# A decoder layer in one program: the scheduler gets a table of hand-over latencies, the first weight tiles wait for input tiles, the late constants and two gate pieces change place

## The chip, the cores and the metric

The kernel runs on one Trainium2 chip, on all 8 cores. Every core computes the whole layer for one sequence of the batch, with no traffic between the cores. The time is the device time of the slowest core in microseconds. Of several executions the median is taken.

## What is computed

A hybrid decoder layer on x of 8 x 2048 x 1024 float32, cut to what matters here:

```python
x = x + 0.5 * swiglu(rmsnorm(x, ffn1_norm), w1, w3, w2)     # 1024 -> 2816 -> 1024
h = rmsnorm(x, mix_norm)
u = h @ w_in                                                 # q, k, v, ret gate, lru x, lru gate
ret = head_groupnorm(retention_chunkwise(rotary(q), rotary(k), v), ret_gn)
y_ret = (silu(g_ret) * ret) @ w_ret_o
hl = rg_lru(causal_depthwise_conv(x_lru, conv_w, conv_b), ...)
y_lru = (hl * gelu(g_lru)) @ w_lru_o
gates = sigmoid(h @ w_branch_gate + b_branch_gate)
x = x + (gates[..., :D] * y_ret + gates[..., D:] * y_lru) @ w_out
x = x + cross_attention(rmsnorm(x, xattn_norm), rmsnorm(mem, mem_norm))
x = x + 0.5 * swiglu(rmsnorm(x, ffn2_norm), ...)
out = rmsnorm(x, final_norm)
```

## The kernel before

Each core holds its sequence as 16 tiles of 128 tokens, in four blocks (tb) of 512. The program is recorded first as a list of operations with the memory that each reads and writes (`Prog.add`), and then put in an order for each engine by a list scheduler.

**The scheduler.** `Prog.schedule` plays the program through with a cost for each operation. Of the operations whose inputs are there it takes the one that can start first on its engine, and among equals the one with the longest path behind it. It also gives out the 8 PSUM banks. What an operation of another engine waits for is taken to be ready `SEM_NS` = 70 ns after its end, whatever the two engines are. A DMA costs its bytes by `DMA_NS_PER_B` plus `DMA_LAT`. Three passes more use the due times of the pass before (`latest`) as keys of the DMAs. The pass with the shortest modelled span gives the order, and that order is fixed in the program: each engine works strictly through its list, POOL (GpSimd) and SP (SyncE) with the DMAs that they issue in it too.

**FFN, up stage** (`FFN.up`, `unit`). The product with W1 and W3 is done for two blocks at a time by a scheme that needs 7 products where 8 are plain. A product is four matmuls of 128x512 (L751, `bank<-hTh,WS` or `bank<-SUM,WS`). A unit is one hidden chunk m of 22 for one pair p of blocks: 7 products, 28 matmuls, on three banks. Three of them go to one bank after another, with a copy of the bank by ACT (L767, `EV<-bank`) in between, so the next product of that bank waits for the copy; others wait for an addition on DVE (L1062). The weights of chunk m lie in one of five slots (`NSLOT`, tiles `WS`): two halves loaded by POOL's queue (L780, 512 KB in HBM each), and four subtractions (L1017, `WS<-WS`), on DVE for the first `TDVE` = 2 chunks and on POOL for the rest. `SUM` tiles are sums over halves of the normalised input (`sums`, L1033). Pair 0 runs `LEAD` = 3 units ahead of pair 1.

**Start.** SP loads the 16 tiles of x and the row of norm weights. ACT squares and sums (`n1JK`), POOL raises to the power -1/2 (`stat`, L949), DVE scales (`n1HB`, L957), PE transposes (L970). `load13` takes for the first three chunks a list of x tiles that must have landed before the halves are loaded; chunks 3 and 4 have no such list.

**Constants.** `consts_late` makes masks, decay tables and bias columns: some 90 small operations, most of them on DVE (L825 to L890), recorded behind the norm of the first FFN.

**FFN, down stage** (`FFN.down`): 704 matmuls `bank<-W,HID`, in pairs of banks for each token tile; at tiles 4 to 11 it carries one of eight side jobs (four `rope_piece`, four `centre_v`). The weights W of this stage and the first weights of the mixer (`LW`) are loaded by POOL's queue.

**Mixer.** 16 steps u of the recurrent branch (`stA`, `stB`, `stG`; `XL`, `XC`, `XCB`, `LW`) run interleaved with the retention steps (`qk`, `gate_`, `block`; weights `RW`), with 16 pieces of the branch gates (`gate_piece`, weights `GW`; `GSCHED` says how many after which step) and the products for the memory attention (`mem_jobs`, `XW`). A tile of the normalised input comes into `hT` by a DMA transpose on SP's queue for tiles below `TR1` = 16, so for all of them. Then come the output products (`tail`, weights `TW`), the cross-attention and the second FFN.

Of the kernel before, what the change touches and what calls it, by code (L numbers as in the profile page):

```python
# [20 lines left out]
SEM_NS = 70.0  # L21
DMA_NS_PER_B = 1.0 / 300.0
DMA_LAT = 2500.0
# [46 lines left out]
class Prog:  # L70
# [42 lines left out]
    def schedule(self, plan=None):  # L113
# [10 lines left out]
        for op in reversed(ops):  # L124
            m = 0.0
            for x in op.succ:
                if bl[x.id] > m:
                    m = bl[x.id]
            bl[op.id] = m + op.cost + (DMA_LAT if op.dma else 0.0)
            op.key = -bl[op.id]  # L130
        for op in ops:
            if op.tie is not None:
                op.key = min(op.key, op.tie.key)
        if plan is not None:
# [33 lines left out]
        def can_take(op):  # L168
# [12 lines left out]
            return b, freeat[b] + SEM_NS  # L181
# [8 lines left out]
        def dma_gate(op):  # L190
# [4 lines left out]
            for x in w:  # L195
# [3 lines left out]
                t = x.fin + SEM_NS  # L199
# [32 lines left out]
        while n:  # L232
# [83 lines left out]
    def latest(self, plan):  # L316
# [14 lines left out]
        for op in sorted(ops, key=lambda o: (-st[o.id][0], -o.id)):  # L331
            dur = op.cost + op.dma * DMA_NS_PER_B + (DMA_LAT if op.dma else 0.0)
            m = span - dur
            for x in op.succ:
                v = ls[x.id] - (0.0 if x.eng == "pe" and op.eng == "pe" else SEM_NS) - dur
                if v < m:
                    m = v
            for i in later[op.id]:
                v = ls[i] - SEM_NS - dur
# [230 lines left out]
TR1 = 16  # L570
# [6 lines left out]
GSCHED = [0, 1, 1, 1, 1, 2, 2, 1, 1, 1, 1, 1, 1, 1, 1, 0]  # L577
# [3 lines left out]
LEAD = 3  # L581
TDVE = 2
# [43 lines left out]
def record(stage, plan):  # L626
# [90 lines left out]
    IOI = A.buf("IOI", 136 * KB, I32, 256)  # L717
    IOF = A.buf("IOF", 137 * KB, F32, 3 * 256)
    WVS = A.buf("WVS", 8 * KB, F32, KC * 256)
    WVB = A.buf("WVB", 16 * KB, BF16, KC * 256)  # L720
    WVM = A.buf("WVM", 20 * KB, F32, KC)
# [33 lines left out]
    def act(out, in_, func, reads, writes, n, tab=None, bias=None, scale=None, accum=None):  # L755
# [8 lines left out]
        if accum is not None:  # L764
            kw["accum_out"] = accum
            nap += 1
# [44 lines left out]

    io_i = IOI.v()
# [15 lines left out]
    def consts_late(gate):  # L828
        dve(lambda e: e.memset(onesb.ap, 1.0), [], onesb.hs, 128)

# [167 lines left out]
    class FFN:  # L998
# [3 lines left out]
        def __init__(self, which):  # L1002
            self.which = which
            self.n13 = 0
            self.units = 0

        def load13(self, after=((), ())):
# [8 lines left out]
            for d, x, y in ((t3, b22, b12), (b12, b12, b11), (t2, b22, b12), (t4, b21, t2)):  # L1016
# [76 lines left out]

        def up(self, side=()):
            bk = Banks(P, 2)
            side = list(side)
            self.sums(0)
            done = [0, 0]

            def go(p):  # L1100
# [3 lines left out]
                self.unit(m, p, bk)  # L1104
# [5 lines left out]
            self.sums(1)  # L1110
            while done[1] < NM:
# [739 lines left out]
```

How the kernel before makes its waits and increments, by code:

```python
            def run(ename, eng):  # L441
                waited = {}
                for op in order[ename]:
                    ws = {}
                    for d in waits[op.id]:
                        if d.dma:
                            s, v = dsem[d.eng][d.idx % NDMASEM], 16 * (d.idx // NDMASEM + 1)
                        else:
                            s, v = esem[d.eng], d.semval
                        if waited.get(id(s), 0) >= v:
                            continue
                        waited[id(s)] = v
                        ws[id(s)] = (s, v)
                    for (s, v) in ws.values():
                        eng.wait_ge(s, v)
                    if op.fn is None:
                        continue
                    ins = op.fn(eng)
                    if op.dma:
                        ins.then_inc(dsem[ename][op.idx % NDMASEM], 16)
                    elif op.marked:
                        ins.then_inc(esem[ename], 1)
```

## Time and profile before

| | |
|---|---|
| median of 3 runs | 1794.6 us (1788.92, 1794.6, 1797.78) |
| the profiled execution | 1786.93 us, span of its slowest core (core 7) 1785.6 us |
| spans of the 8 cores | 1770.6 to 1785.6 us |
| PE busy | 1658.7 us, 93% of the span, 7928 matmuls |
| DVE, ACT, POOL busy | 51%, 44%, 40% of the span |
| chain that ended last | PE 80%, DMA 6%, issue 5%, DVE 4%, ACT 3%, POOL 2% |

An engine's busy time is the time in which it has an instruction in work. Matmuls overlap: one of 128x512 is shown as 379 ns long, while the next one may start much earlier, so short waits of PE are partly hidden in its busy time. The granted clock (PEclk) is 1.00 for 2.4 GHz and 0.50 for 1.2 GHz; in between it is a mean over a stretch.

### The profile page before, as it was taken

The numbers are of one execution on the slowest core, as the hardware profiler recorded it, in microseconds if no ns is written. First come the engines' busy times: TensorE is split into PE (matmuls) and PEld (weight loads), VectorE is DVE, ScalarE is ACT, GpSimd is POOL, SyncE is SP. The second block draws the span as 40 slices with busy tenths as digits, with TensorE's granted clock in tenths as the row PEclk, the third lists the DMA queues.
The fourth block names the chain that finished last, engine by engine and source line by source line (L and its number), as shares of the span: only waits on it lengthen the run. The fifth ranks groups of instructions, "written<-read, shape, count | busy, mean of one in ns | idle before, by whom it ended". The sixth has DMA issues, their size and how long they took to land.

```text
span 1785.6 us, 24375 instructions; the slowest of 8 cores (1770.6 to 1785.6 us)
## 1 busy us (share of the span) xinstructions
PE 1658.7 (93%) x7928; PEld 756.0 (42%) x7928; DVE 911.9 (51%) x1306; ACT 791.2 (44%) x1258; POOL 718.8 (40%) x715
## 2 busy tenths in 40 slices
PE   2899999999979998999997988999999999999998
PEld 1443344344434544444443433444444444444443
DVE  5845644358566544656656423366476444442322
ACT  4544444212146675485675623335444444442111
POOL 5566565401135433443534424323015666653000
PEclk9999999999999998999999999999999999999999
DMA  9232223878984555732101366164444323246332
GB/s 230 54 48 42 30 42 60 141 192 238 204 154 78 94 102 101 162 68 52 38 22 24 67 170 159 36 212 84 134 135 104 42 39 45 42 66 129 131 118 83
DMA packets 111756, 177.27 MB, mean 99 GB/s; under 512 B 49680, under 2 KB 61968, under 8 KB 109584
## 3 DMA queue, kind: packets, MB, share of 16 engines
q0 software_dynamic: 31680, 62.40, 24.1%
q1 hardware_dynamic: 79952, 113.31, 21.0%
q8 instruction: 66, 1.08, 0.2%
q14 instruction: 58, 0.48, 0.1%
HBM read 185.64 MB, written 41.94 MB: 127 GB/s over the span
## 4 chain that ended last, share of the span: by engine, by line
PE 80%; DMA 6%; issue 5%; DVE 4%; ACT 3%; POOL 2%; DVEq 0%; POOLq 0%; ACTq 0%; SPq 0%
PE bank L751 78%; DMA WS<-f_w 2%; DMA XW<-w_xqT 1%; DVE EV L1062 1%; POOL ATP L1530 1%; DMA CS<-rope 1%; DMA W<-f_w 1%; DVE XC L1317 0%; DMA LW<-w_lru_in 0%; ACT L767 0%; PE bank L970 0%; DMA RW<-w_g 0%; DMA XW<-w_xk 0%; DMA TW<-w_tail 0%; POOL QK L1398 0%
## 5 line engine op out<-in xcount | busy, mean ns | idle before, releaser
L751 PE MATMUL bank<-hTh,WS 128*128 128x512 f16 x1408 | 339.5, 382 | 8.6 <-DVE cst L889 2.6
L751 PE MATMUL bank<-W,HID 128*128 128x512 bf16 x1408 | 306.2, 380 | 3.4 <-DMA W<-f_w 3.4
L1062 DVE TENSOR_TENSOR EV<-bank,EV 128x512 f32<-128x512 f32 x264 | 181.8, 690 | 225.9 <-PE bank L751 138.7
L751 PE MATMUL bank<-SUM,WS 128*128 128x512 f16 x1056 | 264.0, 380 | 10.4 <-ACT EV L767 3.7
L751 PEld LDWEIGHTS bank<-hTh,WS 128*128 128x128 f16 x1408 | 136.5, 98 | 183.0 <-issue 27.4
L1017 POOL TENSOR_TENSOR WS<-WS 128x512 f16<-128x512 f16 x160 | 193.5, 1211 | 46.8 <-DMA WS<-f_w 31.6
L751 PEld LDWEIGHTS bank<-W,HID 128*128 128x128 bf16 x1408 | 138.0, 98 | 171.3 <-issue 6.7
L767 ACT ACTIVATE EV<-bank 128x512 f32<-128x512 f32 x264 | 155.5, 590 | 105.3 <-PE bank L751 100.1
L949 POOL TENSOR_TENSOR stat<-stat,cst 128x1 f32<-128x1 f32 x82 | 53.4, 653 | 358.8 <-DVE stat L948 358.6
L767 ACT ACTIVATE EV<-EV 128x512 f32<-128x512 f32 x176 | 110.5, 629 | 192.9 <-DVE EV L1062 188.2
L751 PEld LDWEIGHTS bank<-SUM,WS 128*128 128x128 f16 x1056 | 95.8, 97 | 157.0 <-issue 58.7
L1092 POOL TENSOR_TENSOR HID<-EV,EV 128x512 bf16<-128x512 f32 x88 | 112.2, 1276 | 104.4 <-ACT EV L767 103.1
L751 PE MATMUL bank<-hT,GW 128*128 128x512 bf16 x512 | 121.3, 386 | 7.2 <-DVE GU L1559 3.0
L751 PE MATMUL bank<-hT,RW 128*128 128x512 bf16 x512 | 117.0, 380 | 7.0 <-ACT RS L767 3.3
L751 PE MATMUL bank<-hT,LW 128*128 128x512 bf16 x512 | 116.9, 383 | 6.0 <-DVE T L1395 5.1
L1317 DVE SCALAR_TENSOR_TENSOR XC<-XL,pc,XC 128x1024 f32<-128x1024 f32 x48 | 66.8, 1391 | 68.9 <-ACT XL L767 67.1
L1141 DVE SCALAR_TENSOR_TENSOR XR<-bank,XR 128x512 f32<-128x512 f32 x64 | 43.0, 687 | 103.9 <-PE bank L751 97.9
L1085 DVE TENSOR_TENSOR HID<-bank,EV 128x512 bf16<-128x512 f32 x88 | 60.7, 690 | 54.9 <-PE bank L751 53.0
L1615 DVE SCALAR_TENSOR_TENSOR TT<-TT,bank 128x512 f32<-128x512 f32 x64 | 43.6, 687 | 79.3 <-PE bank L751 73.8
L751 PEld LDWEIGHTS bank<-hT,GW 128*128 128x128 bf16 x512 | 50.0, 99 | 67.4 <-issue 14.7
L751 PEld LDWEIGHTS bank<-hT,RW 128*128 128x128 bf16 x512 | 49.7, 98 | 66.6 <-issue 10.7
L751 PEld LDWEIGHTS bank<-hT,LW 128*128 128x128 bf16 x512 | 50.0, 98 | 65.5 <-issue 9.1
(192 smaller groups left out, 2263.0 us busy)
## 6 DMA issues: line engine op xcount, KB each, us to landing
WS<-f_w POOLq DMA_DIRECT2D x88, 256.0 KB, 4.4
W<-f_w POOLq DMA_DIRECT2D x44, 256.0 KB, 4.9
X<-x SPq DMA_DIRECT2D x16, 512.0 KB, 8.5
XR<-x SPq DMA_DIRECT2D x16, 512.0 KB, 4.8
park<-XR SPq DMA_DIRECT2D x16, 512.0 KB, 4.9
gate_scr<-GU SPq DMA_DIRECT2D x64, 128.0 KB, 2.1
GIN<-gate_scr SPq DMA_DIRECT2D x8, 1024.0 KB, 6.4
X<-park SPq DMA_DIRECT2D x16, 512.0 KB, 5.1
```

Source lines behind the costliest of these rows:

```text
L751: ins = e.matmul(out_ap, l, r, start=(start and i == 0), stop=(stop and i == n - 1), skip_group_check=skip)
L767: P.add("act", lambda e: e.activation(out, in_, func, **kw), reads=reads, writes=writes, cost=act_cost(n, nap), tab=tab)
L949: pool(lambda e: e.tensor_tensor(s[:, 2:3], s[:, 1:2], cc(2), ALU.pow), hs + cst.hs, hs, 550)
L1017: f = (lambda e, d=d, x=x, y=y: e.tensor_tensor(d.ap, x.ap, y.ap, ALU.subtract))
L1062: dve(lambda g: g.tensor_tensor(e.ap, banks[bank][:, :], e.ap, ALU.add), [hbk[bank]] + e.hs, e.hs, TB)
L1085: dve(lambda g: g.tensor_tensor(ha, bv, e1v, ALU.mult), [hbk[al]] + e1.hs, hha, TB)
L1092: pool(lambda g: g.tensor_tensor(hb_, e2v, e4v, ALU.mult), e2.hs + e4.hs, hhb, pool_cost(TB))
L1141: dve(lambda e, b=bs[half], xv=xv: e.scalar_tensor_tensor(xv.ap, banks[b][:, :], 0.5, xv.ap, ALU.mult, ALU.add), [hbk[bs[half]]] + xv.hs, ...
L1317: dve(lambda e, s=s: e.scalar_tensor_tensor(xc.ap, XL.v(s, 1024).ap, pcol("conv_w", s * 8 + c), xc.ap, ALU.mult, ALU.add), xl_all.hs + xc. ...
L1530: pool(lambda e, sa=sa, da=da, rb=rb: e.tensor_tensor(da, sa, rb, ALU.mult), src[0].hs + src[1].hs + rs.hs, dh_[0].hs + dh_[1].hs, pool_co ...
L1615: dve(lambda e, t=t, by=by: e.scalar_tensor_tensor(t.ap, t.ap, 1.0, banks[by][:, :], ALU.add, ALU.mult), t.hs + [hbk[by]], t.hs, TB)
```

## The change

Five edits. (1) The scheduler takes the hand-over time from a table by pair of engines, where it took 70 ns for all: 262 ns from PE to ACT, 272 ns from PE to DVE, 146 ns from any engine to PE, 60 ns within an engine, 100 ns behind a DMA. It takes DMAs as slower too. (2) All five first chunks of weights wait for x tiles (`G13`), and their 20 subtractions are on DVE (`TDVE` = 5, before 2, which made 8). (3) `consts_late` becomes the first side job of the down stage, and every other side job moves back by one token tile; the scratch tiles of the two move to free memory. (4) Pair 0 of the up stage leads by 4 units (`LEAD`). (5) Two gate pieces get their own space and are recorded ahead of step 0 (`EARLY`), and `GSCHED` takes them from steps 1 and 2. The last two tiles of `hT` are transposed by PE (`TR1` = 14). `plain`, `NPLAIN`, `SEED` and `JIT` are switched off.

```diff
-SEM_NS = 70.0
-DMA_NS_PER_B = 1.0 / 300.0
-DMA_LAT = 2500.0
+DMA_NS_PER_B = 1.0 / 240.0
+DMA_LAT = 3000.0
+LAT = {("pe", "act"): 262.0, ("pe", "dve"): 272.0, ("act", "dve"): 140.0, ("dve", "act"): 95.0, ("dve", "pool"): 145.0,
...
+def lat(op, eng):
+    if op.dma:
+        return 100.0
+    if op.eng == eng:
+        return 0.0 if eng == "pe" else 60.0
+    if eng == "pe":
+        return 146.0
+    return LAT.get((op.eng, eng), 280.0 if op.eng == "pe" else 150.0)
...
-                lat = 0.0 if (s.eng == "pe" and e == "pe") else SEM_NS
-                if end + lat > s.ready:
-                    s.ready = end + lat
+                w = end + lat(op, s.eng)
+                if w > s.ready:
+                    s.ready = w
...
-TR1 = 16
+TR1 = 14
...
+EARLY = 2
-GSCHED = [0, 1, 1, 1, 1, 2, 2, 1, 1, 1, 1, 1, 1, 1, 1, 0]
+GSCHED = [0, 0, 0, 1, 1, 2, 2, 1, 1, 1, 1, 1, 1, 1, 1, 0]
...
-LEAD = 3
-TDVE = 2
+LEAD = 4
+TDVE = 5
+G13 = [(1, 3), (5, 6), (7, 8), (9, 10), (12, 14)]
...
-    for i, o in enumerate((56, 16, 96)):
+    for i, o in enumerate((56, 16, 96, 24, 32)):
...
-    f1.load13((x0(1).hs, x0(3).hs))
-    f1.load13((x0(5).hs, x0(5).hs))
-    f1.load13((x0(7).hs, x0(7).hs))
-    gate = x0(15).hs
+    for i, j in G13:
+        f1.load13((x0(i).hs, x0(j).hs))
...
-    consts_late(gate)
...
-    side = []
+    side = [lambda: consts_late([])]
...
+    for i in range(EARLY):
+        gp(*pieces.pop(0), 3 + i)
```

What the change does to the order is seen at three places. The first is POOL's list at the start of the program (WS_51 to WS_55 are the five weight slots, chunk 0 in WS_51; f_w the weights in HBM; stat the powers of the norm). Before:

```order
L780 DMA WS_54<-f_w 128x1024 x2
L780 DMA WS_55<-f_w 128x1024
L818 IOTA IOI 128x128
L837 IOTA IOI 128x16
L857 IOTA IOI 128x1
L780 DMA WS_55<-f_w 128x1024
L1017 TENSOR_TENSOR WS_54<-WS_54 128x512
L949 TENSOR_TENSOR stat<-stat,cst 128x1 x2
L780 DMA WS_51<-f_w 128x1024
L1017 TENSOR_TENSOR WS_54<-WS_54 128x512 x2
L949 TENSOR_TENSOR stat<-stat,cst 128x1
L1017 TENSOR_TENSOR WS_55<-WS_55 128x512
```

And of the change:

```order
L843 IOTA IO_98 128x128
L975 TENSOR_TENSOR stat<-stat,cst 128x1
L804 DMA WS_51<-f_w 128x1024
L975 TENSOR_TENSOR stat<-stat,cst 128x1 x2
L804 DMA WS_51<-f_w 128x1024
L975 TENSOR_TENSOR stat<-stat,cst 128x1 x2
L804 DMA WS_52<-f_w 128x1024
L975 TENSOR_TENSOR stat<-stat,cst 128x1
L804 DMA WS_52<-f_w 128x1024
L975 TENSOR_TENSOR stat<-stat,cst 128x1
L804 DMA WS_53<-f_w 128x1024
```

Before, the halves of chunks 3 and 4 go first, ahead of those of chunk 0, and their subtractions stand among the powers. In the change the halves come in the order of the chunks, one by one between the powers, and no subtraction stands there.

The second place is PE's list in the steady part of the first up stage (bank numbers shown; SUM0 and SUM1 belong to pair 0 and pair 1, WS0 to WS4 are the slots). Before:

```order
L751 MATMUL bank1<-hTh_46,WS3_54 128x512 x4
L751 MATMUL bank5<-SUM1_58,WS0_51 128x512 x4
L751 MATMUL bank1<-SUM0_57,WS3_54 128x512 x4
L751 MATMUL bank7<-hTh_46,WS0_51 128x512 x4
L751 MATMUL bank1<-SUM0_57,WS3_54 128x512 x4
L751 MATMUL bank4<-hTh_46,WS3_54 128x512 x4
L751 MATMUL bank3<-hTh_46,WS3_54 128x512 x4
L751 MATMUL bank6<-hTh_46,WS1_52 128x512 x4
L751 MATMUL bank3<-hTh_46,WS3_54 128x512 x4
L751 MATMUL bank6<-SUM1_58,WS1_52 128x512 x4
```

And of the change:

```order
L775 MATMUL bank3<-SUM1_58,WS0_51 128x512 x4
L775 MATMUL bank2<-hTh_46,WS4_55 128x512 x4
L775 MATMUL bank1<-hTh_46,WS4_55 128x512 x4
L775 MATMUL bank6<-hTh_46,WS1_52 128x512 x4
L775 MATMUL bank3<-SUM1_58,WS0_51 128x512 x4
L775 MATMUL bank7<-SUM0_57,WS4_55 128x512 x4
L775 MATMUL bank6<-SUM1_58,WS1_52 128x512 x4
L775 MATMUL bank5<-hTh_46,WS1_52 128x512 x4
L775 MATMUL bank7<-SUM0_57,WS4_55 128x512 x4
L775 MATMUL bank6<-SUM1_58,WS1_52 128x512 x4
```

Before, one product stands between two on the same bank (bank 1, bank 3, bank 6). In the change there are at least two. Counted over a whole up stage, a product with only one other between it and the one whose bank had to be copied or added first comes 71 times in the first FFN and 76 times in the second before, and 2 times and never in the change. The price is that three units are open at a time, where two were.

The third place is PE's list where the mixer starts, behind the last product of the down stage. Before:

```order
L751 MATMUL bank<-hT,LW 128x512 x16
L751 MATMUL bank<-hT,RW_120 128x512 x32
L751 MATMUL bank<-XCB,LW 128x512 x4
L751 MATMUL bank<-hT,LW 128x512 x32
L751 MATMUL bank<-hT,RW_120 128x512 x32
L751 MATMUL bank<-RW_120,hT 128x512 x8
```

And of the change:

```order
L775 MATMUL bank<-hT,LW 128x512 x16
L775 MATMUL bank<-XCB,LW 128x512 x4
L775 MATMUL bank<-hT,LW 128x512 x16
L775 MATMUL bank<-hT,GW_147 128x512 x16
L775 MATMUL bank<-hT,LW 128x512 x8
L775 MATMUL bank<-hT,RW_121 128x512 x32
L775 MATMUL bank<-hT,GW_147 128x512 x8
```

The 32 matmuls of RW that stood between the first 16 of LW and the 4 on XCB have moved behind them, and the early gate pieces (GW_147, and GW_149 further on) stand among the rest.

In POOL's list for the down stage, four loads of LW stood among the loads of W before, three of them ahead of its last eight. In the change all of W is loaded first. In the output products, the last 48 matmuls of gate pieces in one row are now split in rows of 16 and 24, and between the last of them and the first use of the weights TW that are loaded behind them there are now 16 matmuls, where there were 8.

## Rows read from the trace of the kernel before

**Rows 1.** Stretches, core 7: length, busy (count) by engine, PEclk, DMA share, GB/s.
```profile
45.00:75.00 30.00, 25.89 (x150) 12.43 (x151) 28.64 (x37) 18.23 (x32) 14.55 (x14) 0.91 0.23 68
75.00:170.00 95.00, 93.10 (x417) 38.88 (x416) 43.00 (x66) 44.17 (x76) 59.10 (x58) 1.00 0.28 40
170.00:200.00 30.00, 24.42 (x102) 9.61 (x101) 25.96 (x77) 13.94 (x24) 18.16 (x17) 0.94 0.20 30
200.00:345.00 145.00, 143.20 (x644) 60.59 (x642) 62.10 (x92) 63.98 (x110) 83.37 (x88) 1.00 0.45 72
345.00:360.00 15.00, 12.21 (x48) 5.04 (x49) 1.34 (x3) 0.00 (x0) 5.33 (x9) 0.89 0.84 124
360.00:500.00 140.00, 139.98 (x649) 63.54 (x650) 89.25 (x138) 24.99 (x44) 16.16 (x26) 1.00 0.86 215
...
545.00:1000.00 455.00, 419.58 (x2185) 208.84 (x2183) 259.67 (x328) 288.88 (x419) 197.11 (x163) 0.97 0.37 73
...
1380.00:1600.00 220.00, 216.27 (x968) 90.84 (x967) 94.25 (x137) 100.36 (x174) 138.84 (x136) 1.00 0.31 45
```

**Rows 2.** Chain that ended last, first up stage: start, length, what.
```profile
121.57 7.07 PE bank L751 x32
...
134.40 7.07 PE bank L751 x32
```

**Rows 3.** Timeline, first up stage: start, length, instruction, idle before and releaser.
```profile
142.73 0.60 ACT L767 ACTIVATE EV<-bank 128x512 f32<-128x512 f32 x1 [1.43 <-PE bank L751]
...
143.47 1.02 PE L751 MATMUL bank<-SUM,WS 128*128 128x512 f16 x4
```

**Rows 4.** The page's DMA issues: KB each, median us to landing.
```profile
WS<-f_w POOLq DMA_DIRECT2D x88, 256.0 KB, 4.4
```

**Rows 5.** DMA queues from 0 to 60 us: packets, MB, share of 16 engines.
```profile
q1 hardware_dynamic: 2592, 8.96, 46.3%
q0 software_dynamic: 1440, 2.62, 32.6%
```

**Rows 6.** Timeline of the start.
```profile
1.55 1.76 POOL L780 DMA_DIRECT2D WS<-f_w  x3 [0.85 <-POOLq L627]
...
18.75 6.04 DVE L957 SCALAR_TENSOR_TENSOR n1HB<-X,stat,n1ROW 128x1024 f16<-128x1024 f32 x3 [1.47 <-DMA n1ROW<-rows]
...
46.92 1.87 PE L751 MATMUL bank<-SUM,WS 128*128 128x512 f16 x4 [3.71 <-DVE stat L948]
```

**Rows 7.** Tile WS from 0 to 60 us: ns min/median/max.
```profile
L1017 POOL TENSOR_TENSOR WS<-WS x12: 1139/1300/2131, 11.7 to 53.3; 128x512 f16<-128x512 f16 x12
...
L1017 DVE TENSOR_TENSOR WS<-WS x7: 408/416/1375, 30.9 to 50.6; 128x512 f16<-128x512 f16 x7
```

**Rows 8.** Timeline, constants in the first up stage.
```profile
195.25 3.61 PE L751 MATMUL bank<-hTh,WS 128*128 128x512 f16 x16 [2.64 <-DVE cst L889]
```

**Rows 9.** Timeline, POOL and PE where the down stage starts.
```profile
342.80 0.59 POOL L780 DMA_DIRECT2D W<-f_w  x1 [5.49 <-DMA LW<-w_lru_in]
...
347.47 12.21 PE L751 MATMUL bank<-W,HID 128*128 128x512 bf16 x48 [3.07 <-DMA W<-f_w]
```

**Rows 10.** Timeline, start of the mixer.
```profile
495.56 3.62 PE L751 MATMUL bank<-hT,LW 128*128 128x512 bf16 x16
...
506.04 1.02 PE L751 MATMUL bank<-XCB,LW 128*128 128x512 bf16 x4
...
511.07 0.69 DVE L1393 TENSOR_TENSOR T<-bank,CS 64x512 f32<-64x512 f32 x1 [6.09 <-DMA CS<-rope]
...
517.75 3.57 PE L751 MATMUL bank<-hT,LW 128*128 128x512 bf16 x8 [5.07 <-DVE T L1395]
...
533.97 0.81 PE L751 MATMUL bank<-XCB,LW 128*128 128x512 bf16 x3 [3.78 <-POOL XCB L1320]
```

**Rows 11.** Timeline, PE in the output products.
```profile
1056.18 1.89 PE L751 MATMUL bank<-hT,GW 128*128 128x512 bf16 x8 [1.01 <-DVE GU L1559]
...
1077.18 3.14 PE L751 MATMUL bank<-ATP,TW 128*128 128x512 bf16 x7 [6.03 <-DMA TW<-w_tail]
```

More of the change, by code:

```diff
@@ L133, in schedule @@
                 op.key = min(op.key, op.tie.key)
+        if JIT:
+            rnd = np.random.RandomState(SEED).rand(len(ops))
+            for op in ops:
+                op.key += JIT * rnd[op.id]
         if plan is not None:
@@ L180, in can_take @@
             b = min(free, key=lambda x: (freeat[x], x))
-            return b, freeat[b] + SEM_NS
+            return b, freeat[b] + 146.0
         avail = {e: [] for e in ENGS}
@@ L809, in load_row @@
         return v
+    io_0 = IO0.v()
     io_i = IOI.v()
@@ L1005, in __init__ @@
             self.units = 0
+            self.late = []
         def load13(self, after=((), ())):
@@ L1015, in load13, with wsum @@
             t2, t3, t4 = (s.v(i * 512, 512) for i in (4, 5, 6))
-            for d, x, y in ((t3, b22, b12), (b12, b12, b11), (t2, b22, b12), (t4, b21, t2)):
+            self.pend = [(t3, b22, b12), (b12, b12, b11), (t2, b22, b12), (t4, b21, t2)]
+            if self.which or m >= NPLAIN:
+                self.wsum(m)
+            else:
+                self.late.append((m, self.pend))
+        def wsum(self, m, pend=None):
+            for d, x, y in pend or self.pend:
                 f = (lambda e, d=d, x=x, y=y: e.tensor_tensor(d.ap, x.ap, y.ap, ALU.subtract))
@@ L1092, in unit, with plain @@
             pool(lambda g: g.tensor_tensor(hb_, e2v, e4v, ALU.mult), e2.hs + e4.hs, hhb, pool_cost(TB))
+        def plain(self, m, t, bk):
+            s = WS[m % NSLOT]
+            u = self.units
+            self.units += 1
+            e1 = EV[(u % 3) * 3].v()
+            b1, b3 = bk.next(), bk.next()
+            for r, b in ((0, b1), (1, b3)):
+                wv = s.v(r * D, KC, 128)
+                for hf in range(2):
+                    c = slice(hf * 256, (hf + 1) * 256)
+                    mm_group(banks[b][:, c], b, [(wv.ap[:, k, :], hTh.v((t * KC + k) * TB, TB).ap[:, c]) for k in range(KC)],
+                             wv.hs + hhs(t, hf), cols=256)
+            act(e1.ap, banks[b1][:, :], AF.Silu, [hbk[b1]], e1.hs, TB, tab=S_SILU)
+            f = HID[t].v(0, 4, NM * 128).ap[:, :, m * 128:(m + 1) * 128]
+            hs = []
+            for j in range(4):
+                hs += HID[t].v(j * NM * 128 + m * 128, 128).hs
+            bv = banks[b3][:, :].rearrange("p (j c) -> p j c", j=4)
+            ev = e1.ap.rearrange("p (j c) -> p j c", j=4)
+            dve(lambda g: g.tensor_tensor(f, bv, ev, ALU.mult), [hbk[b3]] + e1.hs, hs, TB)
         def up(self, side=()):
@@ L1096, in up @@
             side = list(side)
+            npl = NPLAIN if self.which == 0 else 0
+            for t in range(2):
+                for m in range(npl):
+                    self.plain(m, t, bk)
             self.sums(0)
@@ L1103, in go @@
                     self.load13()
-                self.unit(m, p, bk)
+                if p or m >= npl:
+                    self.unit(m, p, bk)
                 done[p] += 1
@@ L1110, in up @@
             self.sums(1)
+            for m, pend in self.late:
+                self.wsum(m, pend)
             while done[1] < NM:
```

35 lines of the change are left out of this document (21 added, 14 removed).

## Prediction

> **What bounds the kernel now.** I read the stretches first, because PE is busy 93% of the span and a sum over all of it hides where the rest lies. In the down stage nothing holds PE: 649 matmuls in 140 us, 0.216 us each [rows 1]. With this number, length less count times 0.216 is what PE loses in any stretch that holds matmuls of 512 columns alone, also where the busy time shows no gap. It gives 4.9 us from 75 to 170, 8.0 from 170 to 200, 5.9 from 200 to 345, 4.6 from 345 to 360 and 10.9 us from 1380 to 1600 [rows 1]. In the mixer the widths are mixed, and I take idle time: 455 less 419.6 is 35.4 us from 545 to 1000 [rows 1], and around that stand single waits, 5.07 and 3.78 us ahead of it and 6.03 behind [rows 10, 11]. The start costs 46.9 us until the products with SUM begin [rows 6], with only 80 short transposes and 8 matmuls ahead of them. So what can be won is spread: some 30 us in the two up stages, some 55 in the mixer and the tail, some 35 at the start.
>
> Then the chain, for the steady part of the up stage: it repeats every 12.83 us (134.40 less 121.57) [rows 2], and 2 units hold 56 matmuls, 12.10 us. 0.73 us is lost per two units, with PE at full clock. The timeline says where. An ACT copy of a bank runs from 142.73 to 143.33, and the next product of that bank starts at 143.47 [rows 3]. So a hand-over to PE costs 0.14 us, and the copy itself 0.60, while one product in between covers 0.86. The scheduler counted 0.07 each way and took one product as enough.
>
> **The change, part by part.** The sum is made against the profiled execution, 1786.93 us; the median of the runs is 1794.6, so I take the sum off that.
>
> *Order of products in the up stages.* From PE's last matmul to the copy, the copy, and back to PE takes about 0.26 + 0.60 + 0.14 = 1.0 us (the 0.26 is the change's own number, and the lost 0.2 per place bears it out: 1.0 less 0.86 is 0.14). Two products cover 1.7. With no place left where one product stands between, the short waits go. What they cost in both stages is 4.9 + 5.9 + 10.9 = 21.7 us, and a normal share of the stretch from 170 to 200. I keep 2 us as a rest that has other causes.
>
> *LEAD = 4.* With a lead of 4 all five slots are in use, so a slot is loaded again only when its last unit is done. In the new order ten places, five in each up stage, have 4.3 to 6.8 us of products between the last reader of a half and the first product that needs a subtraction on what replaced it, and about a dozen more per stage 8.5 to 11.9; before none has under 18. The refill needs 4.4 us for the landing [rows 4], 1.2 to 1.3 for a subtraction [rows 7], and whatever stands ahead of it in POOL's list (HID products, and DMA issues that wait for PE): 6 to 9 us. Bounds: nothing, or 3 us at each of the ten tight places, 30. The ten miss the middle of 6 to 9 by about a microsecond, the others mostly hold: I take 8 us for both stages.
>
> *Constants.* 8.0 us is lost from 170 to 200, where DVE is busy 26 of 30 us [rows 1] and PE waits for its constants, once for 2.64 us [rows 8]; the mean rate elsewhere is 1.5 per 30 us, so 6.5 belongs to them. In the down stage they are hidden: PE needs DVE only once per token tile of 9.5 us, and DVE is busy 89 of 140 us there [rows 1]. The cover holds as long as DVE stays under that. ACT has nothing to do there. Up stages together: 21.7 - 2 + 6.5 - 8 = **18 us** gained, ends 0 and 28.
>
> *Start.* Queue shares put a price on transfers: 16 tiles of x and the row of weights took 46.3% of 60 us, 1.63 us each with all engines; ten weight halves took 32.6%, 1.96 us each [rows 5]. Of the first five halves four are for chunks 3 and 4, needed last. POOL issues the first three at 1.55 us, and the row of norm weights lands only at 18.75, after which DVE starts to scale [rows 6]. With the gates these four come behind the tiles: 4 x 1.96 = 7.8 us that the eighth tile no longer waits for. The total is the same, but by then PE has four units of pair 0 to do instead of three. I take **8 us**, ends -5 and 12.
>
> The 12 subtractions that go from POOL to DVE cost DVE 12 x 0.416 = 5.0 us in a stretch in which it is busy 28.6 of 30 us [rows 1, 7]. One took 1.375 us [rows 7], which gives 16.5 us as the upper end. The Trainium skill's GPSIMD Engine Reference (section Specifications) speaks against this edit: it says that GpSimd shares its SBUF interfaces with VectorE and that they contend when a DVE instruction has two SBUF inputs, as these have. The spread from 0.408 to 1.375 for one shape agrees. By the rule DVE would pay up to the 16.5 us and by the median row 5.0; but the same rule takes pressure off, since POOL's own 12 subtractions leave this stretch too.
>
> *W before LW.* POOL waits 5.49 us for a load of LW before it issues the next W at 342.80, and PE then stands for 3.07 us [rows 9]; with the low clock after it (0.89) this is the 4.6 us from above. In the new order this is gone: **4 us**, ends 0 and 4.6.
>
> *Start of the mixer.* Before, 32 matmuls of RW fill the time from 499.2 until XCB is ready at 506.04 [rows 10]. In the new order nothing stands there: PE waits **7 us** for copy, convolution on DVE and cast, and pays the low clock behind it. After a 5.07 us wait 8 matmuls took 3.57 us, 1.7 more than at full rate [rows 10]. That is a loss of 8.7. In return PE no longer stands on banks whose eviction waited for the rope tables (DVE waited 6.09 us for them, PE 5.07 [rows 10]), because SP has two transposes less in front of them and the gate pieces fill in, and the wait of 3.78 at 533.97 has more work ahead of it. With the low clock behind the first this is up to 5.1 + 3.8 + 1.8 = 10.7. Net gain **2 us**, ends -7 and 8.
>
> *Tail.* Gate pieces in a row cost PE about 1.0 us each, five times, and TW then lands 6.03 us late [rows 11]. Split rows and one product more as cover (1.7 us) give **3 us**, ends 0 and 6. The other 35 us of idle time in the mixer depend on a new order that I can't price: 0, ends -15 and +20.
>
> Sum: 18 + 8 + 4 + 2 + 3 = 35 us. 1786.9 - 35 = 1752 for an execution like the profiled one, and 1794.6 - 35 = **1760 us** for the median.
>
> **Rivals.** (a) The truer latencies also shorten the mixer: 35.4 us idle there, of which the upper end of 20 comes back: 1740. For it: its waits end on the same ACT and DVE hand-overs. Against it: they are single, long ones. Chance 0.14. (b) The refill eats the up stages' gain: 2.7 us at each of the ten places instead of 8 us in all, 19 us more: 1779. For it: POOL works strictly in order, and a DMA issue that waits for PE holds the subtractions behind it. Against it: POOL is busy 83 of 145 us [rows 1]. Chance 0.13. (c) DVE bounds the start and gives back its gain, by the shared interface: 8 + 5, 1773. Chance 0.08. (d) The change does not do what it says: the short waits come back as longer ones, and the new 7 us wait stays: no change, 1786 to 1803. For it: the scheduler's model is still a model. Chance 0.07. (e) Slower: POOL becomes the bound of the up stages. Two units take 12.83 us, of which POOL works 83.4 / 145 x 12.83 = 7.4 [rows 1]. If waits in its list waste 6.7 us per two units, the period is 14.1, 1.3 more. Over some 40 periods that is 51 us lost, against 6.5 + 8 + 4 + 2 + 3 = 23.5 that the other parts give: 1822. It decides from a period of about 13.7, where the loss of 33 is 9 more than the gain. Chance 0.04. The forecast itself has 0.54.
>
> **How the numbers follow.** The likeliest case gives 1760. The range takes in (a), (b) and (c) and leaves out (d) and (e) and the far side of (a): 1736 to 1785. A measurement of this kernel can tell some 0.5%, 9 us, from no change (its runs spread over that). Faster by more than that, under 1785.6: 0.54 + 0.14 + 0.13 + 0.08 = 0.89, less a little of (b), 0.88; the same 0.08; slower 0.04.
>
> **What would show it.** The stretch of the steady up stage: a period near 12.1 to 12.3 us for two units; if (b) holds, waits of PE named POOL WS or DMA WS, 1 to 3 us long, about every 36 us. The first product with SUM near 39 us, and the row of norm weights landed by 12. No wait for constants before the down stage, no wait W<-f_w at its start. A new wait POOL XCB of about 7 us right behind the first 16 matmuls of LW. In the output products a wait for TW of 4 us. I would be wrong above all by the mixer, where 55 us of waits are ordered anew, and by POOL's list in the up stages.

## The result: slower by 0.5%, where a gain of 35 us was forecast

| | before | changed |
|---|---|---|
| median of 20 runs each | 1793.34 us | 1804.2 us |
| ratio, 95% interval | | 1.0051 (1.0033 to 1.0069) |
| profiled execution, span of its slowest core | 1786.93, 1785.6 us (core 7) | 1804.28, 1802.6 us (core 0) |
| mean granted clock of the cores | 0.981 to 0.990 | 0.953 to 0.970 |

Forecast were 1760 us, 1736 to 1785. Executions in which all four cores of a die ran at a lower clock for most of the time occur with both kernels; medians count them, ratios leave them out, and the other executions are called undisturbed below.

The first view to read is that of the cores. Of the changed kernel (core, span, mean granted clock):

```profile
core 0: 1802.6 us, clock 0.953
core 1: 1785.2 us, clock 0.958
core 2: 1771.2 us, clock 0.970
...
core 7: 1778.5 us, clock 0.963
```

No core had less than 0.981 before. The program is the same on all cores, and the one with the lowest clock is the slowest by 31 us over the one with the highest. The stretches of core 0 answer to [rows 1] (columns as there):

```profile
75.00:170.00 95.00, 89.35 (x368) 38.02 (x368) 42.23 (x61) 38.35 (x65) 47.67 (x48) 0.90 0.25 37
...
200.00:345.00 145.00, 140.62 (x599) 60.89 (x598) 57.71 (x85) 63.04 (x108) 84.12 (x88) 0.92 0.35 53
...
360.00:500.00 140.00, 139.28 (x632) 63.21 (x644) 86.37 (x192) 23.90 (x44) 21.11 (x34) 0.99 0.77 179
1380.00:1600.00 220.00, 211.87 (x930) 92.94 (x929) 90.16 (x134) 97.75 (x167) 132.39 (x131) 0.95 0.26 40
```

Before, PE did 417, 644 and 968 matmuls in the three stretches of the up stages, at a granted clock of 1.00. Now it does 368, 599 and 930, at 0.90, 0.92 and 0.95. The down stage, as dense as before, keeps 0.99 (its 632 recorded matmuls go with 644 weight loads, against 649 and 650; some matmul records are missing in this trace). Cut finer, the same core shows what such a mean is made of:

```profile
132.00:139.80 7.80, 7.80 (x38) 3.56 (x37) 2.30 (x4) 4.41 (x8) 3.98 (x4) 1.00 0.20 34
139.90:154.80 14.90, 14.90 (x58) 6.20 (x57) 6.37 (x10) 5.51 (x9) 8.42 (x9) 0.81 0.22 35
154.90:165.40 10.50, 10.50 (x50) 4.78 (x49) 4.77 (x8) 5.25 (x9) 2.25 (x4) 1.00 0.30 45
165.50:180.40 14.90, 13.86 (x54) 5.60 (x53) 4.19 (x7) 5.94 (x11) 13.13 (x13) 0.81 0.27 40
180.50:189.20 8.70, 8.70 (x42) 3.89 (x40) 5.23 (x9) 3.41 (x6) 3.20 (x4) 1.00 0.21 31
189.30:204.30 15.00, 15.00 (x59) 6.23 (x58) 3.92 (x6) 7.67 (x13) 7.03 (x7) 0.81 0.17 27
```

These are bouts of a third level, 0.81, between 2.4 and 1.2 GHz. In the first of them PE is busy throughout and gets 58 matmuls into 14.9 us where the full clock would allow 69; in the second it also waits 1.04 us. The trace of the kernel before has no such bout on any core. This one has 18 on core 0, 267.7 us in all, of which 135.2 lie in the first up stage and 105.2 in the second. Two cores each share their bouts: 0 and 1 have 268 and 266 us, 2 and 3 have 150, 4 and 5 have 190, 6 and 7 have 171. On cores 0 to 3 nearly all are 15.0 us long (18 and 10 of them); on cores 4 to 7 they are shorter and more, 32 or 36 of 3.5 to 10.1 us. At 3/16 of their length, since the clock is 13/16 in them, they are worth 28 to 50 us by estimate.

The new waits stand where they were forecast (timeline of PE on core 0: start, length, instruction, idle before and releaser):

```profile
40.90 1.87 PE L775 MATMUL bank<-SUM,WS 128*128 128x512 f16 x4 [2.53 <-DVE SUM L1067]
...
128.12 4.22 PE L775 MATMUL bank<-hTh,WS 128*128 128x512 f16 x11 [4.43 <-POOL WS L1051]
...
516.93 1.87 PE L775 MATMUL bank<-XCB,LW 128*128 128x512 bf16 x4 [6.87 <-POOL XCB L1383]
...
1082.89 1.44 PE L775 MATMUL bank<-ATP,TW 128*128 128x512 bf16 x3 [8.40 <-DMA TW<-w_tail]
```

The first product with SUM comes at 40.9 us instead of 46.92 [rows 6]; W is no longer waited for at the start of the down stage; the wait for XCB is 6.87 us where I had predicted 7. The wait for TW grew from 6.03 to 8.40 instead of shrinking to 4. By groups, PE's waits in the up stages are now for the subtractions on the weights:

```profile
L775 PE MATMUL bank<-hTh,WS 128*128 128x512 f16 x1408 | 359.8, 405 | 19.8 <-POOL WS L1051 18.0
```

### The profile page after: what moved, and what is told of

Read it like the earlier page. It is cut to its first block, busy times and chain, and to the rows that moved or that the text cites. A ratio compares the mean times of both kernels' runs of the same rounds, so it can differ in the third digit from the quotient of the medians.

```text
span 1802.6 us, 24348 instructions; the slowest of 8 cores (1771.2 to 1802.6 us)
## 1 busy us (share of the span) xinstructions
PE 1680.9 (93%) x7838; PEld 776.5 (43%) x7944; DVE 905.5 (50%) x1331; ACT 791.2 (44%) x1256; POOL 681.8 (38%) x692
## 4 chain that ended last, share of the span: by engine, by line
PE 84%; issue 4%; DMA 3%; DVE 3%; ACT 3%; POOL 2%; DVEq 0%; POOLq 0%; ACTq 0%; SPq 0%
PE bank L775 82%; DVE XC L1380 1%; POOL HID L1126 1%; POOL WS L1051 1%; DMA TW<-w_tail 1%; DMA WS<-f_w 1%; PE bank L996 1%; DMA RW<-w_g 1%; POOL ATP L1593 0%; DMA XW<-w_xqT 0%; DVE EV L1096 0%; DMA GW<-w_bgate 0%; DMA X<-x 0%; ACT L791 0%; ACT MU L791 0%
## 5 line engine op out<-in xcount | busy, mean ns | idle before, releaser
L775 PE MATMUL bank<-hTh,WS 128*128 128x512 f16 x1408 | 359.8, 405 | 19.8 <-POOL WS L1051 18.0
L775 PE MATMUL bank<-SUM,WS 128*128 128x512 f16 x1056 | 272.1, 402 | 3.8 <-DVE SUM L1067 3.1
L775 PEld LDWEIGHTS bank<-hTh,WS 128*128 128x128 f16 x1408 | 143.5, 103 | 209.1 <-issue 106.7
L975 POOL TENSOR_TENSOR stat<-stat,cst 128x1 f32<-128x1 f32 x82 | 59.3, 725 | 361.7 <-DVE stat L974 358.2
L775 PEld LDWEIGHTS bank<-SUM,WS 128*128 128x128 f16 x1056 | 107.5, 102 | 143.4 <-issue 66.1
L1051 POOL TENSOR_TENSOR WS<-WS 128x512 f16<-128x512 f16 x136 | 154.8, 1155 | 3.1 <-POOL WS L1051 0.2
L804 POOL DMA_DIRECT2D WS<-f_w x88 | 50.5, 574 | 147.2 <-PE bank L775 136.4
```

What stands on the lines that cost most here:

```text
L775: ins = e.matmul(out_ap, l, r, start=(start and i == 0), stop=(stop and i == n - 1), skip_group_check=skip)
L804: P.add("pool", lambda e: e.dma_start(out=out, in_=in_), reads=reads, writes=writes, cost=600, dma=nbytes)
L975: pool(lambda e: e.tensor_tensor(s[:, 2:3], s[:, 1:2], cc(2), ALU.pow), hs + cst.hs, hs, 550)
L1051: f = (lambda e, d=d, x=x, y=y: e.tensor_tensor(d.ap, x.ap, y.ap, ALU.subtract))
```

## The experiments

The time of a run is that of its slowest core. To see in which stage a change acts, the table gives, as a mean over the 8 cores of each profiled execution, the time from one first matmul to the next: with SUM, with W, with LW, with TW, with SUM again, with W again, last matmul. It is worked out from the start times in the traces. The border between "mixer" and "tail, attention" is the first matmul with TW, and it moves with the order: on core 1, 1482 matmuls follow it up to SUM before, 1488 in e5, 1484 in e6, and 1450 in e8, e9 and e16. Where these differ, only the sum of the two columns can be compared.

| kernel | to SUM | up 1 | down 1 | mixer | tail, attention | up 2 | down 2 |
|---|---|---|---|---|---|---|---|
| before | 47.5 | 291.6 | 156.3 | 516.4 | 327.0 | 277.4 | 152.1 |
| changed, on record | 39.8 | 304.4 | 153.4 | 517.8 | 322.6 | 283.6 | 152.5 |
| changed, again (e5) | 40.2 | 289.4 | 151.9 | 517.5 | 323.1 | 271.5 | 151.7 |
| table alone (e3) | 51.1 | 284.8 | 152.2 | 536.4 | 313.5 | 266.8 | 151.7 |
| 70 ns in the up stages (e4) | 40.1 | 321.0 | 151.9 | 527.4 | 312.8 | 307.5 | 151.7 |
| LEAD = 3 (e6) | 40.4 | 280.5 | 151.9 | 524.9 | 322.9 | 264.9 | 151.7 |
| and EARLY = 0, TR1 = 16 (e8) | 40.4 | 280.6 | 151.9 | 523.2 | 306.8 | 264.8 | 151.7 |
| e8 with TR1 = 14 (e9) | 39.9 | 280.7 | 151.9 | 543.7 | 306.9 | 264.8 | 151.7 |
| e8 with constants early (e11) | 39.5 | 284.9 | 151.9 | 525.7 | 307.4 | 264.8 | 151.7 |
| e8 with the old start (e12) | 50.4 | 279.0 | 151.9 | 522.3 | 306.0 | 267.8 | 151.7 |
| e8 with EARLY = 2 (e16) | 49.8 | 270.6 | 151.9 | 523.6 | 305.6 | 264.8 | 151.7 |

### Zero input for the FFNs (e1, e2)

The edit, in the changed kernel and in the kernel before. It leaves out the FFNs' share of the result: their normalised input, and with it their output, is zero.

```diff
-        dve(lambda e: e.scalar_tensor_tensor(hb.ap, src.ap, r, row.ap, ALU.mult, ALU.mult),
+        dve(lambda e: e.scalar_tensor_tensor(hb.ap, src.ap, r, row.ap, ALU.is_equal if nb.dt is F16 else ALU.mult, ALU.mult),
```

> The changed kernel with the same program, except that the first factor of the FFN norm is a comparison for equality instead of a product, so that the normalised input of both FFNs is zero and their output too (x passes through; the mixer and the attention see almost the same numbers). Theory L (limiter): the bouts of granted clock 0.81, 150 to 268 us per core in the up stages, take about 0.19 of their length, 28 to 50 us, and they come from what the matmuls draw; with zero operands they do not come, the granted clock is 1.00 in the up stages, and the time is about 1804 - 45 = 1760 us. Theory O (order): the time goes to waits in the new order (weight refills 1.6 us at five places a stage, XCB 6.87, TW 8.40) and the 0.81 is only a record: the time stays within 10 us of 1804.

> The kernel before with zero input of both FFNs in the same way. Its trace has no bout of 0.81 on any core. Theory L: nothing to take away, 1793 us within 5. Theory O: the same 1793. A third theory, that zero operands make the FFN faster for another reason, gives a gain here too, as large as in the run on the changed kernel.

Measured: 1760.35 us (ratio 0.9826, 0.9801 to 0.9850) for the changed kernel, without bouts; 1790.48 us (0.9992, 0.9974 to 1.0010) for the one before. It looks as if the limiter theory were proved. It was not: what was missing is the changed kernel with its own data beside it. e5 is that kernel, half an hour later and on another chip than e1 to e4, and it took 1762 us without zeros.

### The table alone, and the old hand-over in the up stages (e3, e4)

e3 puts the function `lat` and the DMA costs into the kernel before, nothing else. e4 sets the hand-overs within a unit of the up stages back to 70 ns (`UP_NS`), in the changed kernel:

```diff
 def lat(op, eng):
+    if op.up:
+        return 0.0 if eng == "pe" and op.eng == "pe" else UP_NS
...
+                    P.up = True
                     self.unit(m, p, bk)
+                    P.up = False
```

> The kernel before with the scheduler's table of latencies and DMA costs alone; the order of the products in the up stages then has no place with one product between (65 and 76 such places before, 0 now). Theory L: the table alone brings the bouts of 0.81 in the up stages, 150 to 270 us per core, 28 to 50 us lost against some 20 won there: slower than before by 5 to 30 us. Theory O: the up stages get shorter by some 20 us and the other edits are what costs: faster by 10 to 20 us, no bouts.

> The changed kernel, but the scheduler counts 70 ns for every hand-over of a product of the up stages, as before; everything else is counted by the table. 50 and 59 places then have one product between again. Theory L: the short waits come back and the bouts go or are fewer than half; 1775 to 1785 us, faster than before by some 10 to 18 (start, constants, W), although PE waits more. Theory O: waits added, nothing won: 1804 + 10 to 20, so 1815 to 1825.

e3: 1774.2 and 1776.6 us in its two undisturbed runs, before beside it 1790.8: 15 us faster, and no bout in its profiled execution, although its up stages were 6.8 and 10.6 us shorter than those of before. That spoke against density as the only cause, as far as a run can without the changed kernel beside it. e4: 1829.3, 1829.4 and 1831.3 us in its three undisturbed runs (ratio 1.0218, 1.0190 to 1.0246), against what either theory expected, and no bout either. The short waits came back in part: of the gaps between the starts of two matmuls from 85 to 335 us, at full clock, 36 are 0.28 to 1 us long (core 5) and cost 6.7 us more than 36 times 0.2154; before there are 52, worth 11.2 us, and in e5 none (core 7 of both). The larger part is long waits for refilled slots, 52.5 us in 12 waits over the whole of core 5, against 18.9 in 10 in e5 (core 7). One of five in the first up stage, core 5:

```profile
218.17 2.29 PE L782 MATMUL bank<-hTh,WS 128*128 128x512 f16 x5 [5.85 <-POOL WS L1058]
```

In the changed kernel the same wait is 1.6 us. The up stages took 31.6 and 36.0 us more than in e5. My reading is that in this order a slot's last reader comes later, so that its refill is late, and that the order with two products between is what makes the lead of 4 bearable. That is argued; no run took the two apart.

### The changed kernel again, LEAD, the number format, the mixer (e5 to e8)

e5 is the changed kernel untouched, e6 has

```diff
-LEAD = 4
+LEAD = 3
```

e7 makes hTh, SUM, WS and the scaled tiles bfloat16 (a coarser input of that product; its diff isn't shown), and e8 is e6 with

```diff
-TR1 = 14
+TR1 = 16
...
-EARLY = 2
-GSCHED = [0, 0, 0, 1, 1, 2, 2, 1, 1, 1, 1, 1, 1, 1, 1, 0]
+EARLY = 0
+GSCHED = [0, 1, 1, 1, 1, 2, 2, 1, 1, 1, 1, 1, 1, 1, 1, 0]
```

> The changed kernel as it is, on the chip of the experiments, because no run so far has it beside one without bouts of 0.81 there: the dense up stages of the kernel with the table alone ran at 1.00 in its profiled execution. Theory L1 (the bouts belong to this program with real data): the bouts are there, clock about 0.96 on all cores, about 1803 us, 42 over the run with zero input. Theory L2 (the bouts belong to the chip, or to its temperature, and not to the program): no bouts here, clock about 0.98 and about 1760 us.

> The changed kernel with LEAD = 3. The slots get their refill earlier again, so the five waits of 1.6 us a stage and the one of 4.4 us for subtractions go, some 14 us. If the bouts come with density alone: they grow, the gain is eaten, 1800 to 1810. If they need something else and do not come: 1745 to 1755.

> The changed kernel with bfloat16 in place of float16 for the up stage's operands (hTh, SUM, WS), same program otherwise; this changes the precision of that part. The down stage, in bfloat16 and as dense, shows no bout in the changed kernel. If the number format or what it switches in the array matters: no bouts, about 1760. If not: as the changed kernel on this chip.

> The changed kernel with LEAD = 3, without the early gate pieces (EARLY = 0, the old GSCHED) and with all tiles of hT transposed by DMA (TR1 = 16). Against the run with LEAD = 3 alone it tells what the parts at the start of the mixer are worth: I expected 2 us of gain from them, ends -7 and +8, so this one is 2 us slower if that was right, and 5 or more faster if the 6.87 us wait for XCB is theirs.

Measured, with before beside them at 1789.89: e5 1762.02 us (0.9838, 0.9807 to 0.9869), e6 1753.12 (0.9793), e7 1760.29 (0.9833), e8 1734.30 (0.9685, 0.9661 to 0.9708). No bout in any of the four traces. The same kernel that was 1804 us is 1762 us here, 28 faster than before. Of its core 7:

```profile
75.00:170.00 95.00, 88.02 (x393) 38.84 (x394) 41.66 (x61) 41.35 (x70) 53.80 (x54) 0.96 0.26 39
170.00:200.00 30.00, 30.00 (x140) 13.49 (x138) 14.70 (x22) 13.81 (x24) 16.43 (x18) 1.00 0.31 46
200.00:345.00 145.00, 140.20 (x649) 63.23 (x649) 56.84 (x85) 61.65 (x105) 86.82 (x92) 1.00 0.45 71
...
1380.00:1600.00 220.00, 211.90 (x980) 95.36 (x979) 94.97 (x141) 102.32 (x175) 136.02 (x139) 1.00 0.36 54
```

PE is as busy as in the recorded trace (211.90 of 220 us, as 211.87 there), but the clock is 1.00 and 980 matmuls fit in where 930 did. What is left to gain is in the idle time: core 7 waits for a subtraction 4.42 us once and then 1.6 us every 38 us:

```profile
123.17 1.44 PE L775 MATMUL bank<-hTh,WS 128*128 128x512 f16 x3 [4.42 <-POOL WS L1051]
...
163.79 1.46 PE L775 MATMUL bank<-hTh,WS 128*128 128x512 f16 x6 [1.60 <-POOL WS L1051]
```

With LEAD = 3 these are gone. There is one new wait, 5.19 us for SUM at 71.6 us (e8, core 0); behind it the up stages run without a gap (0.2154 us per matmul in both rows):

```profile
200.00:345.00 145.00, 145.00 (x673) 65.73 (x672) 55.74 (x84) 58.45 (x100) 83.39 (x92) 1.00 0.52 80
1380.00:1560.00 180.00, 180.00 (x836) 81.58 (x834) 79.11 (x117) 86.69 (x150) 119.10 (x121) 1.00 0.35 54
```

e7 says nothing on whether the number format matters for the bouts, since there was none to take away.

### The parts one by one (e9 to e12, e16)

Each is e8 with one thing put back: TR1 = 14; EARLY = 2 and its GSCHED (e10, and e16 the same again); `consts_late` behind the norm, with its scratch at 136 and 137 KB; and the old start:

```diff
-TDVE = 5
-G13 = [(1, 3), (5, 6), (7, 8), (9, 10), (12, 14)]
+TDVE = 2
+G13 = [(1, 3), (5, 5), (7, 7)]
```

> The best kernel so far (LEAD = 3, EARLY = 0, the old GSCHED, TR1 = 16: 1734.3 us) with TR1 = 14 back, so that the last two tiles of hT are transposed by PE again. It tells which of the two parts cost the 19 us between LEAD = 3 alone (1753.1) and that kernel. If TR1 does: about 1750. If the early gate pieces do: 1734 within 5. In the trace without them the stretch from the first TW product to the second up stage was 306 us instead of 323, so I look there. Should the chip show bouts of 0.81 here, then the limiter theory expects them in the up stages of this kernel and of the other three of this call, and none in the runs of before beside them.

> The same kernel with EARLY = 2 and the changed GSCHED, TR1 = 16. If the early gate pieces cost the 19 us: about 1750. If TR1 does: 1734 within 5. If both are needed for the loss, both runs stay near 1734.

> The same kernel with consts_late back behind the norm of the first FFN (and its scratch tiles at 136 and 137 KB). My term for them was 6.5 us of gain: so 1741, with waits for cst between 75 and 200 us. A rival: in the new order they would hide there too, 1734 within 2.

> The same kernel with the gates and the subtractions of the start as they were (three gated chunks, TDVE = 2). My term was 8 us, and the first product with SUM came at 40.8 instead of 46.9 in the changed kernel: so 1740 to 1744 and the first product with SUM at 47 to 51. A rival: the table of DMA costs alone already orders the start well, 1734 within 2.

Measured, with before beside them at 1791.05: e9 1755.84 us (ratio 0.9808), e10 1729.14 in its one undisturbed run, e11 1739.61 (0.9723), e12 1744.39 (0.9748). All four are set against the 1734.3 of e8, which ran on another chip beside a before of 1789.89, so a microsecond or so of each difference is open. TR1 = 14 costs 21.5 us, all in the mixer (543.7 against 523.2). It costs as much where the early gate pieces are in: e6 and e16 differ in TR1 alone, and 1753.12 stands against some 1731 us. There the loss is seen in the next column (322.9 against 305.6), and the sum of the two is 18.6 us longer, with a wait for TW of 7.88 us on core 1 in e6 that e16 has not. The constants cost 5.3 (the first up stage 4.3 longer), the old start 10.1 (8.4 by the start of the down stage, 3.0 in the second up stage, where the first chunks' subtractions are POOL's again). TR1 = 14 puts a wait on PE at once (e9, core 0):

```profile
485.97 1.86 PE L775 MATMUL bank<-XCB,LW 128*128 128x512 bf16 x4 [8.43 <-POOL XCB L1383]
...
506.08 1.01 PE L996 MATMUL bank<-identb,nxHB 128*128 128x128 bf16 x8 [4.30 <-DVE nxHB L983]
```

The wait for XCB is not part of the loss: e8 has 9.36 us there. The 4.30 us in front of a transpose is new, but e8 has two waits of 4.04 and 5.08 us for QK on the same core that e9 has not. So no single wait explains the loss. On core 1, from LW to SUM, PE is idle for 61.2 us in e9 and 46.7 in e8, and its clock is at 1.2 GHz for 51.2 us against 30.7. The two transposes bring the scheduler into another order. Which rule of it does that was not looked into.

### When the bouts come (e13 to e18)

e13, e15 and e17 are the changed kernel untouched, e14 and e18 the one with zero input, e16 that of e10.

> The changed kernel once more, on whichever chip it lands, to see whether the bouts of 0.81 belong to one chip. Theory C (bouts come on a chip whose limit lies lower, with this program): on such a chip about 1804, clock about 0.96, and the runs of before beside it at 0.98; on another chip about 1762 and 0.98. Theory S (the recorded runs met a passing condition): 1762 wherever it runs.

> The changed kernel with zero input of both FFNs again. Where the kernel with real data has the bouts, theory L expects none here and about 1760; a theory by which the order of the instructions alone brings them expects them here too, about 1800. Where the other has none, 1760 under every theory.

> The changed kernel once more, for one more chip. Theory C: about 1804 and bouts of 0.81 if this chip is of the kind of the recorded runs, 1762 and none if not. Beside it stands a kernel whose up stages are denser still, which must show the bouts too if it does.

> The kernel with LEAD = 3, EARLY = 2, the changed GSCHED and TR1 = 16, which had only one undisturbed run (1729.1 us). I expect 1729 to 1734 again: faster than before by 3.1 to 3.4%. With bouts of 0.81 it would lose at least as much as the changed kernel, some 45 us.

> The changed kernel again, in more rounds. On one chip it ran once at 1762 us and 0.98 on all cores, and later at 1785 to 1789 with two to four cores at 0.965 in seven of eight runs, while before beside it had no such core in its undisturbed runs. If it is a condition of the chip at the time, these runs show the same again (1785 or more in most of them) or none (1760 to 1762), and no mixture; either way more than one run in ten of before does not change with it.

> The same program with zero input of both FFNs, beside it. If the lowered clock is the answer to what the matmuls draw, none of these runs has a pair of cores at 0.965, and they take 1760; if it comes from the order of instructions alone, as many as beside it have.

e13 and e14, on another chip: 1761.0 and 1760.7 us, no bouts. e15, on the very chip of e5: 1786.4 us as the median of eight runs, and in seven of them two to four cores at a clock of about 0.965; before beside it had none such in 17 runs. Theory C, that it takes a certain chip, falls. e16: 1731.1, 1733.1 and 1731.0 us, and 1750.5 with two cores at about 0.974; the ratio, with that run in it, is 0.9691 (0.9634 to 0.9747). e17, on the chip of e1 to e4: all 12 runs have two to six such cores, 1787.5 us (0.9972, 0.9925 to 1.0019), and 7 of 23 runs of before have two. My "no mixture" for before was thus wrong, and so was "more than one in ten does not change". In the profiled execution of e17 cores 2, 3, 6 and 7 have one bout of some 161 us each, from 132 us on, and the others have none. Core 3, then core 0:

```profile
133.00:294.00 161.00, 157.87 (x601) 64.94 (x600) 58.16 (x85) 64.32 (x110) 83.25 (x82) 0.81 0.22 33
```

```profile
133.00:294.00 161.00, 154.59 (x715) 69.48 (x714) 70.73 (x105) 73.34 (x127) 101.11 (x100) 1.00 0.28 42
```

This is the cleanest comparison of the study: same execution, same instructions, same 161 us. Core 3 does 114 matmuls less. Its first up stage takes 316.2 us against 289.0, so the bout costs 27 us. That is 3 us under 3/16 of 161, and PE is idle 3 us less in it (3.13 against 6.41 us): its waits for subtractions, 1.6 us each, are 1.04 in the bout.

e18, with zero input: 1779.7 us; 10 of its 12 runs have a pair of such cores. By its expectation, the order of the instructions would have done it. But its trace shows the bout elsewhere: none in the FFN, where the operands are zero, and one in the mixer, where they are not. Core 4 in the first up stage and in the mixer, then core 2 in the mixer:

```profile
133.00:294.00 161.00, 154.59 (x715) 69.48 (x713) 70.78 (x105) 73.33 (x127) 101.21 (x100) 1.00 0.28 42
528.00:686.00 158.00, 154.80 (x752) 78.39 (x751) 87.96 (x106) 98.00 (x142) 63.10 (x60) 0.81 0.42 81
```

```profile
528.00:686.00 158.00, 147.89 (x857) 79.46 (x856) 97.64 (x118) 110.88 (x166) 74.28 (x69) 1.00 0.48 94
```

So neither side of the expectation was right as written. In this execution the cores with zero operands had no bout in the FFN, and one pair had it in the mixer instead, where the operands are real. That fits a limit on what the matmuls draw, but it is one profiled execution, and in e17 half of the cores had no bout in the FFN with real operands either.

The Trainium skill (TensorE: Matmul & The Clock Gate, section Seeing it yourself) tells of a peak-current limiter that takes a die to 13/16 of the clock once three of its cores run dense matmuls, for as long as the load lasts, and that zero operands do not trip. The level (0.81) agrees, and the FFN of e18 does not speak against it. That it takes the whole die for as long as the load lasts does not fit these bouts: here pairs of cores went down while the others of the same die ran the same program at 1.00, and came back while their own matmuls went on.

## Why the prediction was wrong, point by point

**The sum.** It was 35 us. Where no bout came, the kernel gained 27.9 us (1789.89 to 1762.02), and in the profiled executions 24.7 (1786.93 to 1762.23). So without the bouts the direction and some four fifths of the size held. That 1762 lies so near to the forecast 1760 is partly luck: I took the sum off a median of 1794.6, and before ran at 1790 beside it.

**The step that failed** is the one that has no line in the sum. From [rows 1, 2] I read "0.73 us is lost per two units, with PE at full clock", and took the clock of 1.00 to stay when the waits go. In the recorded executions it did not: the same program in the same order lost 42 us (1804.2 against 1762.0) to bouts of 0.81. That is the slowest core; the mean over the eight cores of the stages together is 1774.1 against 1745.3, 28.8 us more, and 27.1 of them are in the two up stages, where nearly all bouts lie. That cost is shown, by e5 and by the two cores of e17. None of my rivals had it, though one had to end on the slower side and I gave that 0.04.

**Order of products.** Forecast 19.7 us over both stages. e6 against before gives 11.1 and 12.5, less 4.3 for the constants and less 3.0 that the start's `TDVE` gives in the second FFN (e12): 16.3. The table alone gives 6.8 and 10.6, 17.4 (e3). So the mechanism was right, as the short gaps show that went from 52 to none, and the size 2 to 3 us too high.

**LEAD = 4.** Forecast 8 us lost, between 0 and 30. e5 against e6: 8.9 and 6.6, so 15.5, net of the wait of 5.19 us that LEAD = 3 brings. On core 7 the ten tight places are one wait of 4.42 and nine of 1.6 us. With the 6.8 us of cover at the widest of them, a refill takes some 8.4 us by estimate; the middle of my 6 to 9 was 7.5. In whole-kernel time LEAD = 3 gave back only 8.9, because its mixer was 7.4 us longer.

**Constants.** 6.5 forecast, 5.3 measured (e11). That ACT has nothing to do in the down stage was misread: it is busy 25 of 140 us there [rows 1]. No wait came of it. **Start.** 8 forecast, 10.1 measured (e12), 3.0 of it in the second FFN, which I had not thought of: `TDVE` rules there too. **The shared interface** (rival c) did not show: the 17 subtractions on DVE in the first 75 us of e5 took 0.418 us at the median (core 7), as the 0.416 of before. **W before LW.** 4 forecast, 4.4 measured (156.3 to 151.9, e5); the table alone gives 4.1 of it (e3).

**Mixer and tail.** The waits that I summed up as "some 55" us add up to 50.3. Forecast 5 us of gain, measured 2.8 (843.4 to 840.6), a sum of large terms that cancel. The wait for XCB came as forecast. The wait for TW went to 7.9 us (e5) instead of 4. And `TR1` = 14, which I had counted on the gain's side as "SP has two transposes less in front", costs 21.5 us, measured with LEAD = 3 alone. If it costs the same with LEAD = 4, which no run shows, the other edits of the mixer and the new order gave that back. My "0, ends -15 and +20" then hid the largest term of the change.

**Rivals.** (a) did not come: with the table alone mixer and tail took 849.9 us together, against 843.4 before (e3). (d) did not come: the short waits were gone. (b) came in part, at 15.5 us instead of 27. (e) named the right side and the wrong cause: POOL did not become the bound.

**What stays open** is what sets the bouts off. Shown is: they came in the recorded profile, and all 20 recorded executions of the changed kernel have the low mean clock on all cores; on one chip in none of the undisturbed executions and some 40 minutes later in seven of eight; the kernel before, beside e15 and beside e17, had them in 0 of 17 and in 7 of 23 runs. (Where there is no trace, two cores at about 0.965 are taken for a bout.) So the state of the chip matters and the program too. In the program it is not density alone: e16 is denser in the up stages, and beside the seven of eight of e15 it had one such run among four undisturbed ones. e3 and e8 are denser too, but ran when no kernel had bouts. What the profiled bouts of e15, e17 and e18 and the first ones of nearly every core on record have in common is that they begin 4 to 13 us after the clock came back from 1.2 GHz, behind a wait of PE: 4.4 to 4.8 us for a subtraction in e15 and e17 and 3.3 us for a tile in e18. The longest wait in the up stages of e16 is 2.45 us. That points to the step from rest to full work as a trigger. Much speaks against it as the only one. All eight cores of e17 had that wait, and four had no bout. On record, 26 of the 192 bouts of the eight cores begin within 14 us of such a return, and 55 of 81 returns have no bout behind them; the bouts of the second up stage begin when the clock has been off 1.2 GHz for more than 260 us. And no run took away that wait alone under the condition in which the bouts come. So what sets them off is not shown.

The best version is e16, with LEAD = 3, EARLY = 2, TR1 = 16 and everything else of the change: about 1731 to 1733 us in three runs and 1750.5 in a fourth (ratio of the four 0.9691, 0.9634 to 0.9747). e8 lies 3 us from it (ratio 0.9685, 0.9661 to 0.9708), so between these two the choice is open.

## What to carry to other kernels

Look at the granted clock of every core before you explain a difference, and when a change makes PE denser, give the clock a term of its own: a bout at 0.81 costs up to 3/16 of its length, and whether it comes depends on the chip's state as well. A result from one time of measuring can then differ in sign from the next, so run the unchanged kernel beside each experiment, above all beside the one that seems to prove the theory. And price small switches beside the headline edit: the largest loss that one setting made, 21.5 us, was two tiles transposed on another engine.

## What the hardware showed that was not expected

- A granted clock of 0.81, between the two levels, in bouts of 15 us on cores 0 to 3 and of 3.5 to 10 us on cores 4 to 7 (on record), or once for about 160 us (e15, e17, e18), shared by cores 0 and 1, 2 and 3, 4 and 5, 6 and 7. In e15, e17 and e18 other pairs of the same die kept 1.00 meanwhile. One of 161 us cost 27 us in the up stage.
- On record it came almost only in the up stages with float16 operands (240 of 268 us on core 0), and hardly in the down stage in bfloat16, which is as dense. But the bout of e18, 159.8 us, lies in the mixer, whose matmuls are in bfloat16, so it is not float16 alone. The run that would have told formats apart in the FFN (e7) fell into a time without bouts.
- The same program on the same chip: 1762 us, and some 40 minutes later 1786.
